# Ending the second layer's output projection in two column halves for token tile 1

## The reference, cut to what matters

```python
for layer in range(2):
    h = rms_norm(x, g_mix[layer])
    ...                                    # three token mixers, gates
    merged = jnp.sum(gates * y_d, axis=2)
    x = x + merged @ w_out[layer]          # 256 x 1024 times 1024 x 1024
    h = rms_norm(x, g_ffn[layer])
    if layer % 2 == 0: x = x + swiglu(h, ...)
    else:              x = x + moe_ffn(h, ...)

def moe_ffn(h, w_router, w_e_gate, w_e_up, w_e_down):
    logits = einsum('bsd,de->bse', h, w_router)     # 8 experts
    top_vals, top_idx = lax.top_k(logits, 2)
    ...                                             # softmax of the two, weighted sum of expert outputs
```

## Time and profile before

| | |
|---|---|
| Median of 3 runs | 1075.77 us (1074.92 to 1076.01) |
| The profiled execution | 1076.71 us, its span 1074.9 us |
| PE busy | 1054.6 us (98%) |
| DVE, ACT, POOL busy | 813.7 (76%), 670.9 (62%), 116.3 (11%) |
| Chain that ended last | PE 88%, DVE 7%, ACT 3%, issue 1% |
| Output projection of layer 1 to the gathers | about 637 to 672 us of the span |
| Eight experts | 672 to 1065 us |

### The profile page before, as it was taken

The page is one execution under the profiler, slowest core; times in us unless marked ns, Lnnn a source line. Parts: engine busy times, 40 slices in busy tenths (PEclk is TensorE's granted clock), DMA queues, the critical chain, the costliest instruction groups (busy, mean ns, idle before and its releaser), DMA issues.

```text
span 1074.9 us, 16794 instructions
## 1 busy us (share of the span) xinstructions
PE 1054.6 (98%) x6379; PEld 908.1 (84%) x6379; DVE 813.7 (76%) x1142; ACT 670.9 (62%) x946; POOL 116.3 (11%) x131
## 2 busy tenths in 40 slices
PE   8999999999999999999999999999999999999996
PEld 6978788889999999979878888878888888888885
DVE  5679866986545556657967797889898888989884
ACT  5675756555444443556675555857777777878773
POOL 5003330000000000000613000002021020202021
PEclk9999999999999999999999999999999999999998
DMA  9552454567356535345454538789999999999993
GB/s 283 172 187 98 135 180 140 174 204 286 137 195 227 184 140 183 96 151 165 131 185 130 180 142 304 264 270 373 324 370 381 357 342 358 369 383 374 377 371 109
DMA packets 147656, 253.35 MB, mean 236 GB/s; under 512 B 6591, under 2 KB 106005, under 8 KB 147573
## 3 DMA queue, kind: packets, MB, share of 16 engines
q1 hardware_dynamic: 144496, 245.84, 65.8%
q0 software_dynamic: 1296, 4.20, 1.8%
q10 hardware_dynamic: 1780, 2.19, 0.6%
HBM read 248.02 MB, written 4.19 MB: 235 GB/s over the span
## 4 chain that ended last, share of the span: by engine, by line
PE 88%; DVE 7%; ACT 3%; issue 1%; ACTq 0%; POOL 0%; DVEq 0%
PE PS L716 26%; PE PS L1245 11%; PE PS L1246 11%; PE PS L1247 11%; PE PS L1061 6%; PE PS L1063 6%; PE PS L1062 6%; PE PS L821 2%; DVE m_lo L2028 2%; PE PS L740 2%; PE PS L922 1%; DVE w_lo L466 1%; PE PS L1201 1%; DVE scr L2313 1%; DVE big L2305 1%
## 5 line engine op out<-in xcount | busy, mean ns | idle before, releaser
L466 DVE TENSOR_TENSOR w_lo<-ring,w_hi 128x1536 fp32r<-128x1536 f32 (+1 forms) x191 | 310.2, 1633 | 103.8 <-ACT w_hi L457 103.6
L457 ACT ACTIVATE w_hi<-ring 128x1536 fp32r<-128x1536 f32 (+1 forms) x192 | 264.3, 1387 | 117.4 <-PE PS L1063 71.8
L1505 ACT ACTIVATE m_hi<-ring 128x512 fp32r<-128x512 f32 (+2 forms) x256 | 157.7, 631 | 126.2 <-PE PS L716 122.5
L2028 DVE TENSOR_TENSOR m_lo<-ring,m_hi 128x512 fp32r<-128x512 f32 (+2 forms) x256 | 183.0, 744 | 56.9 <-ACT m_hi L1505 54.8
L1245 PE MATMUL PS<-w_hi,hTe 128*96 128x384 f32 (+1 forms) x384 | 125.1, 326 | 0.0
L1246 PE MATMUL PS<-w_hi,hTe 128*96 128x384 f32 (+1 forms) x384 | 124.0, 323 | 0.0
L1247 PE MATMUL PS<-w_lo,hTe 128*96 128x384 f32 (+1 forms) x384 | 123.7, 322 | 0.0
L716 PE MATMUL PS<-m_hi,h_hi 128*128 128x512 f32 (+3 forms) x320 | 119.4, 373 | 1.7 <-DVE m_lo L2028 1.7
L716 PE MATMUL PS<-m_hi,h_lo 128*128 128x512 f32 (+3 forms) x320 | 115.1, 360 | 0.0
L716 PE MATMUL PS<-m_lo,h_hi 128*128 128x512 f32 (+3 forms) x320 | 115.0, 359 | 0.0
L1061 PE MATMUL PS<-h_hi,w_hi 128*128 128x256 f32 x352 | 99.9, 284 | 0.0
(11 more groups left out here) (362 smaller groups left out, 2190.0 us busy)
## 6 DMA issues: line engine op xcount, KB each, us to landing
ring<-in_w_in_dram SPq DMA_DIRECT2D x39, 1024.0 KB, 5.0
ring<-in_w_exp_gate_dram SPq DMA_DIRECT2D x48, 768.0 KB, 7.7
ring<-in_w_exp_up_dram SPq DMA_DIRECT2D x48, 768.0 KB, 8.9
ring<-in_w_exp_down_dram SPq DMA_DIRECT2D x24, 1536.0 KB, 10.1
ring<-in_w_branch_dram SPq DMA_DIRECT2D x12, 1024.0 KB, 5.0
ring<-in_w_ffn_gate_dram SPq DMA_DIRECT2D x12, 768.0 KB, 6.0
ring<-in_w_ffn_up_dram SPq DMA_DIRECT2D x12, 768.0 KB, 6.2
ring<-in_w_ffn_down_dram SPq DMA_DIRECT2D x6, 1536.0 KB, 6.3
```

Source lines behind the costliest of these rows:

```text
L457: act.activation(split_parts(u, j)[0], ring[:, i % NSLOT, w0:w0 + words], ACT.Copy)\
L466: dve.tensor_tensor(lo, ring[:, (j // 2) % NSLOT, w0:w0 + words], hi.bitcast(F32), SUB).then_inc(sem(f"lo_ready{b}"), 1)
L1505: act.activation(hi, raw, ACT.Copy).then_inc(sem("m_hi_ready"), 1)
L2028: dve.tensor_tensor(lo, raw, hi.bitcast(F32), SUB).then_inc(sem("m_lo_ready"), 1)
```

## The change

`last_out` replaces `token_after_token` for `out3` of layer 1. It has three steps: tile 0 with 512 columns, tile 1 with columns 0 to 255 of the half (bank w11), tile 1 with columns 256 to 511 (a new use w12). `out1` of layer 1 also treats tile 1 in two groups of 256 columns, as its sums begin in the same two banks. DVE adds the residual in two parts, PE turns the first two k tiles and then the last two, ACT copies them one pair after the other, and the last router products come in two pairs. `w12` is put into `USES` behind `w11`. `LEAD_ZEROS` goes from (3, 3, 2) to (2, 2, 2); the first of the three now stands between the two pairs of transposes.

```diff
@@ -62,7 +62,7 @@
 TSLOTS = 5
 LOGIT_BANKS = (6, 7)
 EARLY, EARLY_PAIRS = 4, 3
-LEAD_ZEROS = (3, 3, 2)
+LEAD_ZEROS = (2, 2, 2)
 DB = 4
 ROWS_DONE = NE + 1
 
@@ -193,6 +193,7 @@
                "hf00", "hf10", "hf01", "hf11"])
 USES = [(L, u) for L in range(DEPTH) for u in MIX_USES]
 USES[5:5] = [(-1, "par")]
+USES.insert(USES.index((DEPTH - 1, "w11")) + 1, (DEPTH - 1, "w12"))
 
 
 def place_uses():
@@ -1006,17 +1007,38 @@
                                               merged[:, a, (4 * hf + i) * P:(4 * hf + i + 1) * P], ident[:, :])
                         mm.then_inc(full, 1)
 
+                def last_out(opened):
+                    between = {(1, 1): [lambda: turn_h(L, "hf", 0, 1), lambda: logits(0, 0, 4)],
+                               (1, 2): [lambda: logits(0, 4, 8)], (1, 3): [lambda: logits(1, 0, 4)]}
+                    for step, (a, c0, n) in enumerate(((0, 0, 512), (1, 0, 256), (1, 256, 256))):
+                        dst, full = opened[step]
+                        for p in range(PIECES):
+                            for ahead in between.get((step, p), ()):
+                                ahead()
+                            if step == 0:
+                                pe.wait_ge(sem("m_lo_ready"), piece_no(L, "out3", p) + 1)
+                            _, hi, lo = piece_of(L, "out3", p)
+                            t, w = slice(a * P, (a + 1) * P), slice(c0, c0 + n)
+                            for y, (xx, ww) in enumerate(((mg_hi, hi), (mg_lo, hi), (mg_hi, lo))):
+                                mm = pe.matmul(dst[:, w], xx[:, 4 + p, t], ww[:, w], start=False,
+                                               stop=(p == PIECES - 1 and y == 2), skip_group_check=True)
+                            if step == 2 and p < PIECES - 1:
+                                mm.then_inc(sem("piece_used"), 1)
+                        mm.then_inc(full, 1)
                 def out_part(m, opened, ahead={}):
 
                     kh, c = divmod(m, 2)
-                    if m == 3:
-                        token_after_token(L, "out3", [b for b, _ in opened], [f for _, f in opened], mg_hi, mg_lo, 4,
-                                          between={} if L < DEPTH - 1 else {
-                                              (1, 1): [lambda: turn_h(L, "hf", 0, 1), lambda: logits(0, 0)],
-                                              (1, 2): [lambda: logits(0, 1)], (1, 3): [lambda: logits(1, 0)]})
+                    if m == 3 and L == DEPTH - 1:
+                        last_out(opened)
+                    elif m == 3:
+                        token_after_token(L, "out3", [b for b, _ in opened], [f for _, f in opened], mg_hi, mg_lo, 4)
                     else:
-                        by_pieces(L, f"out{m}", [(f, [(b, 0, 512, a)]) for a, (b, f) in enumerate(opened)], mg_hi, mg_lo, 4 * kh,
-                                  ahead=ahead)
+                        groups = [(f, [(b, 0, 512, a)]) for a, (b, f) in enumerate(opened)]
+                        if len(opened) > TT:
+                            groups[1:] = [(f, [(b[:, x * 256:(x + 1) * 256], x * 256, 256, 1)]) for x, (b, f) in enumerate(opened[1:])]
+                        by_pieces(L, f"out{m}", groups, mg_hi, mg_lo, 4 * kh, ahead=ahead)
 
                 def turn_first_half():
 
@@ -1033,7 +1055,7 @@
                 out_part(0, w0, {2: lambda: turn_merged(1, [0]), 3: lambda: turn_merged(1, [1])})
                 evacuated(L, "mt10"), evacuated(L, "mt11")
                 out_part(2, w0)
-                w1 = [begin(L, f"w1{a}") for a in range(TT)]
+                w1 = [begin(L, f"w1{a}") for a in range(TT + (L == DEPTH - 1))]
                 out_part(1, w1, {PIECES - 1: turn_first_half})
                 out_part(3, w1)
                 if L < DEPTH - 1:
@@ -1128,17 +1150,35 @@
                         if a == 0:
                             mm.then_inc(sem("down_full"), 1)
 
-            def logits(a, c):
-                if c == 0:
+            def logits(a, k0, k1):
+                if k0 == 0:
                     pe.wait_ge(sem(f"gate_free{a}"), gate_no(2, 0))
                     pe.wait_ge(sem("router_ready"), 1)
-                evacuated(1, f"hf{a}{c}")
-                for i in range(4 * c, 4 * c + 4):
+                if (a, k1) == (TT - 1, 6):
+                    pe.wait_ge(sem("last_turned_read"), 1)
+                else:
+                    evacuated(1, f"hf{a}{k0 // 4}")
+                for i in range(k0, k1):
                     mm = pe.matmul(PS[:, LOGIT_BANKS[a], 0:NE], hT[:, i, a * P:(a + 1) * P], wr[:, i, :],
                                    start=(i == 0), stop=(i == KD - 1))
-                if c:
+                if k1 == KD:
                     mm.then_inc(sem("logits_full"), 1)
+            def turn_last():
+                bank, full = begin(1, "hf11")
+                for i in range(4):
+                    if i == 0:
+                        evacuated(1, "w11")
+                    if i == 2:
+                        zeros(LEAD_ZEROS[0], USE[(1, "hf00")][0])
+                        pe.wait_ge(sem("last_turned_read"), 1)
+                        evacuated(1, "w12")
+                    mm = pe.transpose(bank[:, i * P:(i + 1) * P], x_tok[:, 1, (4 + i) * P:(5 + i) * P], ident[:, :])
+                    if i == 1:
+                        mm.then_inc(sem("last_half_turned"), 1)
+                mm.then_inc(full, 1)
 
             mixer(0)
             dense(0, first=True)
@@ -1149,17 +1189,17 @@
 
             rank_of = PS[:, LOGIT_BANKS[0], NE:2 * NE], PS[:, LOGIT_BANKS[0], 2 * NE:3 * NE]
             totals = PS[:, LOGIT_BANKS[1], NE:2 * NE]
-            idle_bank = USE[(1, "w10")][0]
+            idle_bank = USE[(1, "hf00")][0]
             LAST_BANK = LOGIT_BANKS[1]
 
             pe.wait_ge(sem("tri_ready"), 1)
             pe.wait_ge(sem("msel_ready"), 1)
             pe.matmul(rank_of[1], ones[:, :], msel[:, 0, :], start=True, stop=False, skip_group_check=True)
             pe.matmul(rank_of[0], tri, msel[:, 0, :], start=False, stop=True, skip_group_check=True).then_inc(sem("rank_full"), 1)
-            zeros(LEAD_ZEROS[0], idle_bank)
-            turn_h(1, "hf", 1, 1)
+            turn_last()
+            logits(1, 4, 6)
             zeros(LEAD_ZEROS[1], idle_bank)
-            logits(1, 1)
+            logits(1, 6, 8)
             for b in range(NB):
                 mixer_left(1, b)
 
@@ -1430,6 +1470,9 @@
                 for c in range(2):
                     _, _, free, n = use(DEPTH - 1, f"w{c}{a}")
                     pool.wait_ge(free, n + 1)
+                if a:
+                    _, _, free, n = use(DEPTH - 1, "w12")
+                    pool.wait_ge(free, n + 1)
                 pool.dma_start(y[:, a, :], x_tok[:, a, :]).then_inc(sem("residual_out"), 16)
             pool.wait_ge(sem("residual_out"), 16 * TT)
 
@@ -1528,7 +1571,9 @@
                 bank, free = full(w // 2, f"{('hm', 'hf')[w % 2]}{a}{c}")
                 x = bank.rearrange("p (k t) -> p k t", t=P)
                 k = slice(4 * c, 4 * c + 4)
-                if w == 2 * DEPTH - 1:
+                if w == 2 * DEPTH - 1 and (a, c) == (1, 1):
+                    act.activation(hT[:, 6:8, a * P:(a + 1) * P], x[:, 2:4, :], ACT.Copy).then_inc(free, 1)
+                elif w == 2 * DEPTH - 1:
                     act.activation(hT[:, k, a * P:(a + 1) * P], x, ACT.Copy).then_inc(free, 1)
                 else:
                     act.activation(h_hi[:, k, a * P:(a + 1) * P], x, ACT.Copy).then_inc(sem("h_hi_ready"), 1)
@@ -1768,6 +1813,11 @@
                 high(w + 1, 0, 1)
                 if L == DEPTH - 1:
                     token_high(0, 1)
+                if L == DEPTH - 1:
+                    act.wait_ge(sem("last_half_turned"), 1)
+                    bank, _, _, _ = use(L, "hf11")
+                    act.activation(hT[:, 4:6, P:2 * P], bank[:, 0:2 * P].rearrange("p (k t) -> p k t", t=P), ACT.Copy)\
+                       .then_inc(sem("last_turned_read"), 1)
                 high(w + 1, 1, 1)
                 if L == DEPTH - 1:
                     token_high(1, 1)
@@ -2337,6 +2387,20 @@
                 split(L, "br11", [2]), merge(2, 3)
                 gated(1, 0), merge(1, 0), gated(1, 1), merge(1, 1)
                 split(L, "br11", [3])
+                def first_of_last():
+                    bank, free = full(L, "w11")
+                    x = x_tok[:, 1, 512:768]
+                    dve.scalar_tensor_tensor(x, bank[:, 0:256], 0.5, x, MUL, ADD).then_inc(free, 1)
+                def rest_of_last():
+                    bank, free = full(L, "w12")
+                    x = x_tok[:, 1, 768:D]
+                    dve.scalar_tensor_tensor(x, bank[:, 256:512], 0.5, x, MUL, ADD).then_inc(free, 1)
+                    freed(L, "w11")
+                    freed(L, "w12")
                 def x_plus(c, a):
                     bank, free = full(L, f"w{c}{a}")
                     x = x_tok[:, a, c * 512:(c + 1) * 512]
```

(5 more changed lines are left out.)

## The result

| | before | changed |
|---|---|---|
| Median (19 runs each) | 1075.84 us (1073.93 to 1077.19) | 1077.30 us (1075.24 to 1080.01) |
| Ratio | | 1.0023, 95% interval 1.0016 to 1.0029 |
| The profiled execution, its span | 1076.71, 1074.9 | 1079.96, 1078.2 |
| PE busy | 1054.6 | 1057.4 |

The time lies in the range (1075.2 to 1078.4), and near the forecast of 1076.9. But where the sum said +1.1 us, the medians lie 1.46 apart, the means of the 19 runs 2.20 (1077.69 against 1075.49), and the ratio comes to 2.5. So the change is slower by about the 0.2% that I had called measurable: the interval, 0.16 to 0.29%, has that on both sides. Half of the loss in the mean is what I worked out. The other half had no term in my sum.

The account below looks back on a forecast made before the run. PE, always busy behind 720 us, was taken as the bound, so shifts of the gathers count fully: 0.95 + 0.15 + 0.02 = +1.12 us. Profiled 1076.71 becomes 1077.8; the median, 0.94 lower, gives 1076.9 us, range 1075.2 to 1078.4.

Parts of the forecast that it names:

- the sum: Shifts from `out1` to the gathers, carried to the end: 0.95 + 0.15 + 0.02 = +1.12 us.
- Part 1: Ahead of `out1`, PE waits until DVE has read w00, whose bank w12 gets: +0.95, bounds 0.80 to 1.05.
- the upper bound: For the wait ahead of `out1`: 1.05, with a restart cost of 0.10 on the first matmul.
- Part 2: Narrow matmuls take 0.120 each, wide ones 0.2275; tile 1's narrow pass in `out1` costs +0.15 (0.0 to +0.4).
- Part 3: End of `out3`: the first narrow piece saves nothing, and bank w12 is full 0.48 later than the whole was.
- Part 4: Last projection matmul to gathers, with halved transposes, copies and router products: 2.80 for 3.26; with Part 3, +0.02.
- Others: Side effects on ACT, POOL, SP's load and the zeros: no term added; 8 zeros cut to 6 leave no gap over 0.5.
- Rival (A): The clock falls behind the new wait before `out1`, near 650: 1.6 more, 1078.5 us, slower by 0.25%; chance 8%.
- Rival (B): The clock's fall in the first expert does not come: -1.6, giving 1075.3 us; chance 9%.
- C: The wait for w00 is cheaper or absent, and the halves bring 0.35: 1075.4 to 1076.2 us; chance 10%.
- D: In `out3`'s end DVE's additions come late and handoffs cost more: about +1 on top, 1077.9 us; chance 8%.

Follow-up runs that it names:

- e8: Changed kernel with nine matmuls of zeros in the first expert's 2.1 us wait, ahead of PE's wait for the weights; median 1076.97 us, ratio 1.0015.
- e2: Kernel before with one more PE wait ahead of `out1`, for DVE's reading of w00; median 1075.96 us, ratio 1.0006.
- e1: Changed kernel with PE's wait for w12's bank moved from ahead of `out1` to where w12 is first written; median 1075.80 us, ratio 1.0004.
- e3: e1 with three narrow pieces of tile 1, not one, ahead of the transposes of tile 0's second half in `out3`; median 1075.05 us, ratio 0.9996.
- after_again: The changed kernel run once more, unaltered, beside the kernel before; median 1076.95 us, ratio 1.0021.
- e5: Changed kernel with three matmuls of zeros in PE's 0.5 us wait for the residual of tile 0; median 1076.76 us, ratio 1.0014.
- e9: e1 with nine matmuls of zeros in the first expert's 2.1 us wait, ahead of PE's wait for the weights; median 1075.73 us, ratio 1.0004.
- e10: e2 with nine matmuls of zeros in the first expert's 2.1 us wait, ahead of PE's wait for the weights; median 1075.47 us, ratio 1.0005.

## Why the prediction was right, and where it was not

The mechanism and every term of the sum can be read in e8's profiled execution, where the clock stays at 1.00 through the stretch. PE's last matmul of out2, the first of `out1`, tile 1's first narrow piece, the last narrow matmul, the ranks, the two pairs of transposes and router products, the gathers:

```profile
648.63 0.39 PE L717 MATMUL PS<-m_lo,mg_hi 128*128 128x512 f32 x1
649.91 0.47 PE L717 MATMUL PS<-m_hi,mg_hi 128*128 128x512 f32 x1 [0.89 <-DVE x_tok L2411]
```
```profile
659.23 0.28 PE L1024 MATMUL PS<-m_hi,mg_hi 128*128 128x256 f32 x1
...
660.26 0.63 PE L679 MATMUL PS<-ident,x_tok 128*128 128x128 f32 x4 [0.53 <-DVE x_tok L2411]
```
```profile
664.59 0.28 PE L1024 MATMUL PS<-m_hi,mg_lo 128*128 128x256 f32 x1
...
665.78 0.28 PE L1024 MATMUL PS<-m_lo,mg_hi 128*128 128x256 f32 x1
665.90 0.28 PE L1197 MATMUL PS<-u,ones 128*128 128x8 f32 x2
...
666.26 0.42 PE L1178 MATMUL PS<-ident,x_tok 128*128 128x128 f32 x2
666.52 0.59 PE L763 MATMUL PS<-zb 128*128 128x512 bf16 x2
667.15 0.44 PE L1178 MATMUL PS<-ident,x_tok 128*128 128x128 f32 x2
667.43 0.51 PE L1163 MATMUL PS<-wr,hT 128*128 128x8 f32 x4
667.79 0.59 PE L763 MATMUL PS<-zb 128*128 128x512 bf16 x2
668.23 0.51 PE L1163 MATMUL PS<-wr,hT 128*128 128x8 f32 x4
668.59 0.45 PE L1216 MATMUL PS<-psel,htok_hi 128*128 128x192 f32 x2
```

- **Part 1** (+0.95, at most 1.05): the mechanism is right, the size 0.10 too small. 648.63 and 0.2275 is 648.86, and `out1` starts at 649.91: 1.05. The number is that of the upper bound, but not for its reason: from the end of DVE's addition to PE's start it took 0.26, and not 0.15. The restart cost comes on top (650.22 - 649.91 = 0.31 to the second matmul of `out1`, for 0.2275) and lies in the +0.64 below. e2 has the wait alone, e1 is without it.
- **Part 2** (0.120 for a narrow matmul): right. Ten of them take 665.78 - 664.59 = 1.19. The Trainium skill's 109 ns ("TensorE: Matmul & The Clock Gate", "Back-to-back issue gap") is not reached here; that section gives its formula for an isolated matmul, and these stand in a stream.
- **Part 3** (+0.48 and +0.15): right. From the first matmul of `out1` to the ranks 665.90 - 649.91 = 15.99, against 664.27 - 648.92 = 15.35 before: +0.64. The first narrow piece saves nothing, the wait for the residual grew from 0.2 to 0.5. With three narrow pieces ahead of the transposes (e3) the wait is gone and the lowest runs are 0.84 under those of e1, so the order loses it, and not the width.
- **Part 4** (2.80 for 3.26): right. 668.59 - 665.90 = 2.69, 0.11 better, mostly because a pair of router products took 0.36 (667.79 - 667.43) and not half of 0.91. The half-width operations took 0.42 on DVE and 0.38 on ACT, as taken:

```profile
664.74 0.42 DVE L2398 SCALAR_TENSOR_TENSOR x_tok<-PS,x_tok 128x256 f32<-128x256 f32 x1 [0.65 <-PE PS L1024]
...
666.10 0.42 DVE L2404 SCALAR_TENSOR_TENSOR x_tok<-PS,x_tok 128x256 f32<-128x256 f32 x1
```
```profile
666.72 0.38 ACT L1823 ACTIVATE hT<-PS 128x256 f32<-128x256 f32 x1 [4.55 <-PE PS L1178]
667.63 0.38 ACT L1579 ACTIVATE hT<-PS 128x256 f32<-128x256 f32 x1 [0.53 <-PE PS L1178]
```

- **Sum**: 1.05 + 0.64 - 0.57 = +1.12, the 1.12 predicted, with two errors of 0.1 that cancel. The two waits of the first expert kept their 2.6 and moved along (in the profile of the changed kernel; here they are filled). So did a wait of 0.27 for `psel` ahead of the second gathers, at 669.96 before, which the prediction left out.
- **The clock in out3 had no term** in the sum, and that is the step that failed. The one sentence that could have raised it, under "Others", is "The zeros lost (8 to 6) leave no gap longer than 0.5." It looks for idle time alone, and behind the stretch in question: in the five profiled executions with a fall at 664 (the changed kernel, after_again, e1, e5, e9) the clock went down between 661.5 and 664.4, and the first of these zeros came at 667.9 or later. So the zeros taken away did not begin it. Idle time is not needed either, as e5 shows. What the changed kernel has between 659 and 664 that the kernel before has not are half-width matmuls, where wide ones stood between transposes and router products of 8 columns. That this thinner work is what the clock answered to is argued, not shown.
- **Rival (A)** had the price (1.6 for 3.4 us) and the wrong place and cause. It put the fall behind the new wait at 650; no profiled execution shows one there, and e10 has 2 of 11. It came at 664, in about half the runs of the changed stretch, where I had given the whole case 8 in 100, and in three of the five profiled executions it lasted about 6.8 us (an estimate from the shares of the stretches).
- **Rival (B)** is real, but as a part of every kernel: the fall in the expert comes in some executions and not in others, before as after. The median of before already holds it. C and D did not happen. That the median came out 0.4 above the forecast is in part luck: both medians are those of runs with one fall, which hides most of the falls that were added; the means do not hide them.

So of a loss of 2.1 us in the mean (1077.70 over 31 runs against 1075.62 over 103), 1.1 is the sum, and about 1.0, what is left, I put down to the more frequent falls. Shown: that they go with the changed stretch. Not shown: which of its parts does it, since the narrow matmuls of `out1`, those of `out3` and the gap of 0.5 were not each tried alone with enough runs.

## What to carry to other kernels

When a use is added to a round-robin list of buffers, look up whose buffer it gets and when that one's last reader is done on its own engine's queue; here that was the one microsecond of the change, and putting the wait where the buffer is first written removed it. Splitting work to start the next engine earlier pays only behind the last wait: the pieces ahead of it must fill it, or they are lost. And since the clock fell here without idle time too (e5), ask also what a change does to the work in a stretch, not only what gaps it leaves, and compare distributions, since one median hides which level it stands on.

## What the runs showed of the hardware

The granted clock fell from 1.00 to 0.50 with PE busy for all 3.00 of each 3 us (e5, 658 to 667), after transposes, 8-column and half-width matmuls; and it fell after 2.1 us of waiting in some executions of one program and not in others. A stretch at the lower level cost 1.6 us in 3.4. Nine matmuls of zeros in a wait that was idle anyway took the number of runs with a mean clock of 0.996 or less from 58 of 103 (18 of 35 on the same chip) to 1 of 12.
